# Split products of a decoder layer on one Trainium2 core: three terms taken in turn for each row block, or one term at a time over all eight

## What is computed

```python
h = rmsnorm(x, norm_mix_g)
(a_u, a_b, a_c, g_q, g_k, g_v, g_z, g_a, g_b, m_q, br_gates) = _split_cols(h @ w_in)
...
merged = (gates[:, :, 0] * (ya @ w_br_conv) + gates[:, :, 1] * (yb @ w_br_gdn)
          + gates[:, :, 2] * (ym @ w_br_mem))
x = x + merged @ w_out
...
q = (xb @ w_q).reshape(blk, PEER_HEADS, 2, PEER_D_HALF)
s = jnp.einsum('nhpd,phkd->nhpk', q, sub_keys).astype(jnp.float32)
sv, si = lax.top_k(s, PEER_TOPK)
...
act = jax.nn.gelu(jnp.einsum('nd,nhkd->nhk', xb, u).astype(jnp.float32), approximate=False)
coef = (gates * act).astype(xb.dtype)
return jnp.einsum('nhk,nhkd->nd', coef, jnp.take(v_tab, eidx, axis=0))
```

## Time and profile before

| what | value |
|---|---|
| median of 3 runs | 4512.43 us (4511.94 to 4512.93) |
| the profiled execution | 4514.07 us |
| its span in the profile | 4512.2 us |
| PE busy, matmuls | 4363.4 us (97%), 28685 |
| PE busy, weight loads | 4258.5 us (94%), 28685 |
| DVE busy | 3027.0 us (67%) |
| ACT busy | 1122.0 us (25%) |
| POOL busy | 2133.7 us (47%) |
| DMA | 911.79 MB, mean 202 GB/s |

### The profile page before, as it was taken

The page is one execution under the profiler, slowest core; times in us unless marked ns, Lnnn a source line. Parts: engine busy times, 40 slices in busy tenths (PEclk is TensorE's granted clock), DMA queues, the critical chain, the costliest instruction groups (busy, mean ns, idle before and its releaser), DMA issues. The chain is left out here.

```text
span 4512.2 us, 75302 instructions
## 1 busy us (share of the span) xinstructions
PE 4363.4 (97%) x28685; PEld 4258.5 (94%) x28685; DVE 3027.0 (67%) x5420; ACT 1122.0 (25%) x2076; POOL 2133.7 (47%) x1529
## 2 busy tenths in 40 slices
PE   8999999999999999999999979987999999999998
PEld 6999999999979999998999979987999999999998
DVE  5123560111126673545788989988999999999998
ACT  3111331111223332114222234432222222222222
POOL 2233222233212322333355468865666666666664
PEclk9999999999999999999999999999999999999999
DMA  5212223433442123534222269999999999999997
GB/s 188 62 56 75 94 90 99 123 110 95 150 149 83 50 56 124 161 119 152 78 82 80 73 224 363 359 353 327 340 355 348 352 351 355 346 355 346 356 345 257
DMA packets 578569, 911.79 MB, mean 202 GB/s; under 512 B 150536, under 2 KB 398344, under 8 KB 578245
## 3 DMA queue, kind: packets, MB, share of 16 engines
q1 hardware_dynamic: 429728, 420.79, 28.2%
q0 software_dynamic: 111744, 406.90, 25.2%
q10 hardware_dynamic: 36928, 81.93, 4.9%
HBM read 775.67 MB, written 133.84 MB: 202 GB/s over the span
## 5 line engine op out<-in xcount | busy, mean ns | idle before, releaser
L2874 PE MATMUL ea_banks<-h_high,ea_uT_high 128*128 128x336 f32 x2048 | 656.1, 320 | 22.5 <-ACT ea_coef L3796 16.5
L2874 PE MATMUL ea_banks<-h_high,ea_uT_low 128*128 128x336 f32 x2048 | 652.0, 318 | 0.0
L2874 PE MATMUL ea_banks<-h_low,ea_uT_high 128*128 128x336 f32 x2048 | 648.2, 316 | 0.0
L134 PE MATMUL p_in<-h_high,w_in_high 128*128 128x352 f32 x1536 | 496.1, 323 | 0.0
L134 PE MATMUL p_in<-h_low,w_in_high 128*128 128x352 f32 x1536 | 492.3, 321 | 0.0
L134 PE MATMUL p_in<-h_high,w_in_low 128*128 128x352 f32 x1536 | 492.0, 320 | 0.0
L2849 POOL DMA_INDIRECT yT<-in_peer_u,gt_index x256 | 334.9, 1308 | 175.3 <-DVE ex_dots L3909 81.7
L2874 PEld LDWEIGHTS ea_banks<-h_high,ea_uT_high 128*128 128x128 f32 x2048 | 388.1, 189 | 24.0 <-ACT ea_coef L3796 16.8
L2849 POOL DMA_INDIRECT ea_u_raw<-in_peer_v,gt_index x192 | 302.4, 1575 | 188.0 <-DVE h_low_plain L3915 130.1
L2874 PEld LDWEIGHTS ea_banks<-h_low,ea_uT_high 128*128 128x128 f32 x2048 | 387.9, 189 | 0.0
L2874 PEld LDWEIGHTS ea_banks<-h_high,ea_uT_low 128*128 128x128 f32 x2048 | 386.6, 189 | 0.0
(11 more groups left out here) (590 smaller groups left out, 11277.3 us busy)
## 6 DMA issues: line engine op xcount, KB each, us to landing
w_in_raw<-in_w_in SPq DMA_DIRECT2D x88, 512.0 KB, 3.6
ex_gate<-tmp_gates SPq DMA_DIRECT2D x64, 672.0 KB
ea_u_raw<-in_peer_uT SPq DMA_DIRECT2D x66, 512.0 KB
w_mb_raw<-in_peer_v SPq DMA_DIRECT2D x64, 512.0 KB
ea_uT_low_plain<-in_peer_uT SPq DMA_DIRECT2D x62, 512.0 KB
ex_lv_low_plain<-in_peer_v SPq DMA_DIRECT2D x62, 512.0 KB
tmp_acts<-ea_coef ACTq DMA_DIRECT2D x64, 336.0 KB
tmp_gates<-yT SPq DMA_DIRECT2D x28, 768.0 KB
```

The lines of the kernel that those rows point to most:

```text
L134: last = pe.matmul(banks[0:rows, n, 0:CH], a[:, kk, 0:rows], b[:, kk, chunk(n)], start=(kk == 0 and a is wt.high[s] and b is high), stop=( ...
L2874: last = pe.matmul(acts.banks[:, n, 0:CD], a[:, c, :], b[:, c, dense(n)], start=(c == 0 and a is acts.uT_high[s] and b is high), stop=(c = ...
```

## The change

The two loops over row blocks and over the three terms change places, in the four lines named above: first all eight row blocks high by high, then all eight with the activation's residual, and then all eight with the weight's residual. `act_chunk` also waits for less at its start (`uT_high_made`, the high half of its tile), and for `uT_low_made` only before the third term; in `multiply` the waits for single blocks stand at the first term.

```diff
     for n in range(NCH):
-        for kk in range(KT):
-            if cut and n == 0:
-                pe.wait_ge(cut[0], cut[1] + kk + 1)
-            if each:
-                pe.wait_ge(each, KT * n + kk + 1)
-            for a, b in ((wt.high[s], high), (wt.high[s], low), (wt.low[s], high)):
+        for a, b in ((wt.high[s], high), (wt.high[s], low), (wt.low[s], high)):
+            for kk in range(KT):
+                if cut and n == 0 and a is wt.high[s] and b is high:
+                    pe.wait_ge(cut[0], cut[1] + kk + 1)
+                if each and a is wt.high[s] and b is high:
+                    pe.wait_ge(each, KT * n + kk + 1)
                 last = pe.matmul(banks[0:rows, n, 0:CH], a[:, kk, 0:rows], b[:, kk, chunk(n)],
...
-                    for kk in range(KT):
-                        for x, v in ((wh, high), (wh, low), (wl, high)):
+                    for x, v in ((wh, high), (wh, low), (wl, high)):
+                        for kk in range(KT):
                             last = pe.matmul(ps_g[:, j % 4, 0:CH], x[:, kk, :], v[:, kk, chunk(n)],
...
     if n == 0:
-        pe.wait_ge(acts.uT_low_made, e + 1)
+        pe.wait_ge(acts.uT_high_made, e + 1)
     if not first:
         pe.wait_ge(acts.chunk_kept, DC * e + n - 1)
-    for c in range(KT):
-        for a, b in ((acts.uT_high[s], high), (acts.uT_high[s], low), (acts.uT_low[s], high)):
+    for a, b in ((acts.uT_high[s], high), (acts.uT_high[s], low), (acts.uT_low[s], high)):
+        if n == 0 and a is acts.uT_low[s]:
+            pe.wait_ge(acts.uT_low_made, e + 1)
+        for c in range(KT):
             last = pe.matmul(acts.banks[:, n, 0:CD], a[:, c, :], b[:, c, dense(n)],
...
-                    for kk in range(KT):
-                        for a, b in ((wt.high[u], high), (wt.high[u], low), (wt.low[u], high)):
+                    for a, b in ((wt.high[u], high), (wt.high[u], low), (wt.low[u], high)):
+                        for kk in range(KT):
                             last = pe.matmul(prod[:, n, 0:CH], a[:, kk, :], b[:, kk, chunk(n)],
```

## The result

The changed kernel is slower, by about 10 us. Its median is 4522.18 us (4516.25 to 4552.05, 21 runs) against 4512.43 us (4504.32 to 4525.15, 21 runs); the ratio is 1.0026, 95% interval 1.0017 to 1.0034. The profiled execution has 4522.18 us, a span of 4520.3 us against 4512.2, so 8.1 us lie between the two traces.

The account below looks back on a forecast made before the run. The prediction took PE's matmul distance to bound most stages, with DVE bounding `experts`. All terms were 0 us, so 4514.07 us stayed 4514.1 for the profiled execution; the forecast median was 4512 us, range 4492 to 4527.

Parts of the forecast that it names:

- What bounds the kernel: PE's distance between matmul starts, set by the moving stream, bounds the stages before `spread_gates`; DVE bounds `experts`.
- price of 10.7 us per ns: At the reordered matmuls that count, 8736 at 352 columns and about 1930 at 336: 1 ns each is worth 10.7 us.
- I take 0 between -0.8 and +1.0 ns: At the reordered matmuls: the new order leaves the distance between starts unchanged; term 0 us, from -8.5 to +10.7.
- slower, by another rhythm: Rival: at reordered matmuls, moving-operand steps cost 1.0 to 1.1 ns more; 4521 to 4527 us with mid-chunk stops; chance 0.22.
- 155.0 ns for `values`: In `values`, the distance read at 336 columns, 1.1 ns over line 2874, used to price the slower rival.
- Faster, by the repeated block: Rival: at reordered matmuls, sharing the next one's weight block is dear, and the new order avoids it; 4492 to 4503 us; 0.22.
- Much faster: Rival: at reordered matmuls, fewer high-low operand changes save 11 ns at 352 columns, 13 at 336; 4391 us; chance 0.07.
- `act_chunk`'s waits: In `act_chunk`: waiting for the high half only gives 0 us; the mid-chunk residual wait gives 0, up to +3.4 us.
- the DVE chain that was said to be late next: Behind the stall at 2565 us: PE waits 11.62 us for DVE's last sorting, so an earlier start gains 0 us.
- the 11.62 us would grow by what the stall lost: Sign of being right: PE's wait before line 3101 grows by what the stall at 2565 us, 2.48 us, lost.
- The first tile of `merge_branches`: In `merge_branches`: PE stands some 0.3 to 0.6 us for DVE's residual blocks, covered by a later wait; term 0 us.
- The first tell-tale: Sign of being right: a window of line 134 in `project_in` shows 158.7 to 159.3 ns a matmul.

Follow-up runs that it names:

- values_by_chunk: The kernel before with `values`' loop over operations and chunks turned round after the first row block, so neighbours move the same chunk; 4510.38 us, ratio 0.9998.
- old_nest_swapped: The kernel before with its nest kept but the terms swapped in line 134, so no two neighbours share a weight block; 4511.52 us.
- same_weight_block: The changed kernel with seven of eight weight blocks left out at line 134, so eight neighbours share one; 4541.6 us.
- after_late_wait: The changed kernel with `act_chunk`'s waits put back: residual waited for at the chunk's start, nothing in mid-chunk; 4530.41 us, ratio 1.0049.
- only_134: The kernel before with the new order in `multiply` (line 134) alone; 4525.07 us, ratio 1.0026.
- after: The changed kernel itself, with the new order at all four lines and the changed waits, against the kernel before; 4522.18 us, ratio 1.0026.
- only_act: The kernel before with the new order in `act_chunk` alone, with its changed waits; 4509.98 us, ratio 1.0001.
- only_gates_queries: The kernel before with the new order in lines 1357 (gates) and 3037 (queries) alone; 4516.49 us, ratio 1.0009.
- same_moving_block: The changed kernel with seven of eight activation row blocks left out at line 134, so the moving operand starts at the same place 24 times; 4518.33 us.
- even_odd: The changed kernel with row blocks taken as 0, 2, 4, 6, 1, 3, 5, 7 at all four lines; 4515.08 us, ratio 1.0006.

## Why the prediction was wrong

- **What bounds the kernel** held. PE's distance is what counts in `project_in`, the gates, the merge and the queries, and `experts` is bound by DVE: a turn stayed at 44.7 us though `act_chunk` got cheaper by 2 ns. A turn does depend on PE in `values`, as values_by_chunk shows. The price of 10.7 us per ns was right in its size, but it took one ns for all sites, and the sites moved in opposite directions.
- **The step that failed** is "I take 0 between -0.8 and +1.0 ns". The shift was +0.6 or +2.6 in `project_in`, +1.8 to +2.5 at the other 352-column sites, and -2.1 at 336 columns in `top_experts`. Both ends of the bound were too near. The lower one came from the durations of the three terms, the upper one from rows that differ in weights, buffers and column counts, while the quantity the change alters, the sequence of the moving operand's starts, was the same in all of them: each start three times or, in `values`, another regular pattern. The text called the three stages "the same shapes and other addresses"; the addresses were others, their sequence was not. In microseconds the term is +8.4 by the table, inside its -8.5 to +10.7, and the median of 4522 us lies inside the stated 4492 to 4527. That is luck: +12.5 us at some places were set against -4.1 at others, and with the slower rhythm of `project_in` the same program took 4532 and 4535 us.
- **The rival "slower, by another rhythm"** is what happened, in its mechanism (the moving operand steps at every matmul); its price was met by luck: it said 4521 to 4527 us from 1.0 to 1.1 ns everywhere, and 4522 came out of +0.6 to +2.5 at some places and -2.1 at another. It had 0.22. Its 155.0 ns for `values` was read from a turn's stretch; the mean distance of its 6048 matmuls is 154.41, 0.5 over line 2874 and not 1.1.
- **"Faster, by the repeated block"** fell in two runs: old_nest_swapped and same_weight_block leave the distance where the nest puts it. The 323, 321 and 320 ns were a phase, as the text allowed: in old_nest_swapped the first matmul of three still lasts 323 ns and the others 321 and 320, though no neighbour has its weight block. **"Much faster"** fell with the change itself, which gave 159.6 to 161.6 and 151.8 ns where it wanted 148 and 141. The two passes of 148 ns were a supposition: the row shows 296 ns a matmul, and no run shows a pass of its own. No load is saved by a shared block here: same_weight_block, with eight neighbours on one block, still shows 28685 loads for 28685 matmuls, and 161.65 ns.
- **`act_chunk`'s waits,** taken as 0: borne out. The stall of 2.48 us became 1.38 in mid-chunk, after_late_wait keeps the changed kernel's distances, and the DVE chain that was said to be late next still ends 59.9 us after the scores (59.8 before). That the 11.62 us would grow by what the stall lost did not show: they read 11.11, since the waits for `h_high_plain` just ahead grew from 2.2 to 3.8 us.
- **The first tile of `merge_branches`,** "0, 0.6 without that cover": borne out, cover and all. The first chunk lost 0.7 us, the 0.45 us for `w_mb_low` are gone, and the tile came out 0.20 us longer, of which 0.18 are the new rhythm.
- **The first tell-tale,** 158.7 to 159.3 ns in `project_in`, read 159.5 in the stretch of the earlier trace rows: just outside, and it would have told little, since two executions of five read 161.7 there.

## What to carry to other kernels

When a change permutes instructions of one kind, ask what sequence it alters (here the starts of the moving operand, which now go on by a row block, 4224 bytes, at every matmul and not at every third), and bound its cost by rows in which that sequence differs; here, rows that differed in everything else gave a bound that was too narrow. Compare distances between starts site by site before summing with one price: two shapes moved in opposite directions, and the version that keeps the new order in `act_chunk` alone, with `values` turned round, ran faster than both kernels. And take more than one profile of a kernel whose times spread more than its neighbour's: one profile of this one would have told a gap of 8 us, another one of 21.

## What the runs showed of the hardware

- **A rhythm of TensorE that locks in.** With 352 columns and starts 4224 bytes apart, the first and third chunks of `project_in` ran at a period of four matmuls with a mean of 158.5 and 158.7 ns in three profiles of the changed kernel and of 161.6 and 161.3 in two (the second chunk at 161.6 or 161.7 in all), from the first matmuls of the stage to its last, some 740 us later. In the old order, three matmuls to a start, the period is six (161, 162, 156, 161, 155, 159) and was 159.0 in every profile. What decides between the two rhythms stays open: the executions differ by a few ns in the first starts, and no run set these on purpose.
- **The start of the moving operand counts, not which weight block is loaded.** With one weight block for eight neighbours `project_in` kept the 161.65 ns of only_134, and with one row block of the activations it had 159.47. Constant starts, in bytes behind the start of `h`'s tile: 160.0 ns at 0 and 2816 and 158.4 at 1408, for 352 columns; 153.7, 153.3 and 153.3 at 1536, 2880 and 5760, and 156.0 at 7104, for 336. Steps of 4224 bytes from 2880 on gave 150.3, less than any constant start tried. Why is open, too. The remainder by 256 is an estimate from the three starts at 352 columns; a tile with padded rows, which would test it, was not run, and steps of one and of two row blocks were not told apart.
- **A sequence spills over.** Line 2376, whose order was never edited, went from 158.88 to 161.13 ns where line 134's order in the same stage was the new one (only_134, after), and stayed where it was not (158.88 and 158.89 in only_act and only_gates_queries), and in same_moving_block and even_odd too (158.90 and 158.91). Its matmuls come 144 or 72 at a time right behind 432 of line 134, which had 161.64 in only_134 and after and 159.09 to 159.47 in the others. That it is only the neighbourhood is not shown by a run of its own.
- **What a pause costs behind it.** In the kernel before, 18 distances at 352 columns behind a pause of 3.27 us were 293 or 294 ns, at a granted clock of 0.53; behind the same pause, 2.49 us long, the changed kernel had some 160 ns and 1.00.
